# The gates of a linear recurrence: both gates of a head side by side in one stationary operand, two heads in the two row halves of TensorE, tanh on 64 partitions at a time

## The reference

```python
def block_diag_linear(x, w, b):            # 16 heads of 64 channels
    xb = x.reshape(bsz, s, LRU_BLOCKS, LRU_BLOCK_W)
    y = jnp.einsum('bsnc,ncd->bsnd', xb, w).reshape(bsz, s, LRU_WIDTH)
    return y + b

def rg_lru(x, w_a, b_a, w_x, b_x, lam):
    r = jax.nn.sigmoid(block_diag_linear(x, w_a, b_a))
    i = jax.nn.sigmoid(block_diag_linear(x, w_x, b_x))
    log_a = -LRU_C * r * jax.nn.softplus(-lam)
    a = jnp.exp(log_a)
    mult = jnp.sqrt(jnp.maximum(-jnp.expm1(2.0 * log_a), 0.0))
    bterm = mult * (i * xf)
    # h[t] = a[t] * h[t-1] + bterm[t]
```

## Time and profile before

| what | value |
|---|---|
| median of 3 runs | 1322.02 us |
| profiled execution: its own time | 1322.41 us |
| profiled execution: span of the trace | 1320.6 us |
| PE busy | 1309.9 us, 99% of the span |
| DVE busy | 917.7 us, 69% |
| ACT busy | 716.3 us, 54% |
| moved by DMA | 233.36 MB, 177 GB/s in the mean |
| load of `lru_w` | one transfer of 1024.0 KB |

### The profile page before, as it was taken

One profiled execution on the slowest core, in us unless ns is written; L12 is line 12 of the kernel. 1 busy time (PEld: TensorE's weight loads), 2 busy tenths in 40 slices (PEclk: granted clock), 3 DMA queues, 4 the chain that ended last, 5 costly groups with the idle time before them and its releaser, 6 DMA issues.

```text
span 1320.6 us, 18090 instructions
## 1 busy us (share of the span) xinstructions
PE 1309.9 (99%) x7220; PEld 1113.3 (84%) x7220; DVE 917.7 (69%) x1113; ACT 716.3 (54%) x1021; POOL 94.1 (7%) x84
## 2 busy tenths in 40 slices
PE   9999999999999999999999999999999999999999
PEld 7788888987788888888888999888888889998887
DVE  6756556687978755546767668876776766698675
ACT  6544445568746544435776444554467664445452
POOL 0000000000101000001252000000002610000000
PEclk9999999999999999999999999999999999999999
DMA  7866637542386866545656543546566564344562
GB/s 262 281 212 199 205 111 243 172 127 81 128 255 207 268 187 187 189 143 159 206 162 199 168 129 115 190 144 181 185 199 216 174 208 145 113 144 144 150 196 85
DMA packets 64243, 233.36 MB, mean 177 GB/s; under 512 B 7456, under 2 KB 7584, under 8 KB 64032
## 3 DMA queue, kind: packets, MB, share of 16 engines
q1 hardware_dynamic: 61488, 223.37, 53.9%
q10 hardware_dynamic: 2672, 8.84, 2.0%
HBM read 231.14 MB, written 1.05 MB: 176 GB/s over the span
## 4 chain that ended last, share of the span: by engine, by line
PE 89%; DVE 5%; DMA 2%; ACT 2%; issue 1%; POOL 1%; ACTq 0%; another core or an unknown queue 0%; POOLq 0%; DVEq 0%
PE psum L1906 22%; PE psum L1927 22%; PE psum L1907 22%; PE psum L1974 5%; PE psum L1912 5%; PE psum L1959 5%; PE psum L1913 5%; PE psum L2122 2%; DMA raw<-weights 2%; PE psum L2345 2%; DVE w_lo L1173 1%; DVE y_lo L1173 1%; PE psum L2223 1%; ACT w_hi L606 0%; ACT y_hi L606 0%
## 5 line engine op out<-in xcount | busy, mean ns | idle before, releaser
L1173 DVE TENSOR_TENSOR w_lo<-raw,w_hi 128x1024 fp32r<-128x1024 f32 x226 | 274.1, 1222 | 125.9 <-ACT w_hi L606 124.1
L606 ACT ACTIVATE w_hi<-raw 128x1024 fp32r<-128x1024 f32 x226 | 237.7, 1057 | 139.9 <-PE psum L1927 104.3
L1906 PE MATMUL psum<-w_hi,x_hi 128*128 128x512 f32 x552 | 218.3, 396 | 1.0 <-ACT w_hi L606 1.0
L1173 DVE TENSOR_TENSOR y_lo<-raw,y_hi 128x1024 fp32r<-128x1024 f32 x144 | 175.3, 1222 | 58.8 <-ACT y_hi L606 57.9
L1907 PE MATMUL psum<-w_hi,x_lo 128*128 128x512 f32 x552 | 214.9, 389 | 0.0
L606 ACT ACTIVATE y_hi<-raw 128x1024 fp32r<-128x1024 f32 x144 | 151.9, 1057 | 80.9 <-PE psum L1927 49.4
L1927 PE MATMUL psum<-w_lo,x_hi 128*128 128x512 f32 x552 | 170.2, 389 | 0.3 <-DVE w_lo L1173 0.3
L1906 PE MATMUL psum<-y_hi,x_hi 128*128 128x512 f32 (+1 forms) x376 | 148.6, 395 | 0.0
L1907 PE MATMUL psum<-y_hi,x_lo 128*128 128x512 f32 (+1 forms) x376 | 146.5, 390 | 0.0
L1906 PEld LDWEIGHTS psum<-w_hi,x_hi 128*128 128x128 f32 x552 | 103.9, 188 | 24.4 <-issue 2.6
L1927 PEld LDWEIGHTS psum<-w_lo,x_hi 128*128 128x128 f32 x552 | 103.7, 188 | 22.6 <-DVE w_lo L1173 1.2
(11 more groups left out here) (204 smaller groups left out, 2327.4 us busy)
## 6 DMA issues: line engine op xcount, KB each, us to landing
raw<-weights SPq DMA_DIRECT2D x422, 512.0 KB, 4.0
arena<-gains ACTq DMA_DIRECT2D x7, 512.0 KB, 4.7
arena<-gate_bias ACTq DMA_DIRECT2D x2, 1536.0 KB, 8.0
res<-x SPq DMA_DIRECT2D x2, 512.0 KB, 5.8
arena<-lru_w ACTq DMA_DIRECT2D x1, 1024.0 KB, 4.8
cst<-consts ACTq DMA_DIRECT2D x1, 736.0 KB, 5.4
out<-res SPq DMA_DIRECT2D x1, 512.0 KB, 2.6
out<-res SPq DMA_DIRECT2D x2, 256.0 KB, 2.0
```

What stands on the lines that cost most here:

```text
L606: act.activation(slot(t)[0], raw[:, t % RAW, :], ACT.Copy).then_inc(hi_ready, 1)
L1173: dve.tensor_tensor(lo, raw[:, t % RAW, :], hi.bitcast(F32), ALU.subtract).then_inc(lo_ready, 1)
L1906: pe.matmul(out_, l_hi, r_hi, start=start, stop=False, skip_group_check=skip)
```

## The change

The stationary operand becomes 128 partitions x 8 feature tiles x 128 columns: on the 64 rows of a head lie its r matrix (64 columns) and its i matrix (64 columns). A matmul takes 64 rows and streams the head's 64 channels x 256 tokens; its result has r on partitions 0 to 63 and i on 64 to 127 for one head. The two heads of a feature tile are in the upper and lower row half and write to the two banks of a pair. A part is now two feature tiles with both gates, no longer four feature tiles with one gate. The counts of matmuls, and of parts, stay.

ACT now has four reads for a feature tile: for each gate and head, 64 partitions x 256. Where gate and head lie in other halves, it writes to other partitions than it reads. Before the decays it waits for its own reads of both parts. The biases are laid out anew, and `lru_w` is half as large.

```diff
-        lru_blocks = view(0, 2, KD, P)
+        lru_blocks = view(0, KD, P)
...
-            act.dma_start(lru_blocks.rearrange("p a f d -> p (a f d)"), lru_w).then_inc(lru_loaded, 16)
+            act.dma_start(lru_blocks.rearrange("p f d -> p (f d)"), lru_w).then_inc(lru_loaded, 16)
...
-            def tanh_part(half, which):
-
-                act.wait_ge(ri_ready, 2 * half + which + 1)
-                fill = (F_R0, F_I0, F_R1, F_I1)[2 * half + which]
-                dst = lru_i if which else lru_a
-                for j in range(4):
-                    f = 4 * half + j
-                    ins = act.activation(dst[:, f, :], pair(fill)[:, j // 2, (j % 2) * SEQ:(j % 2 + 1) * SEQ],
-                                         ACT.Tanh, scale=0.5, bias=half_bias[:, which * KD + f:which * KD + f + 1])
+            def tanh_part(half, part):
+
+                act.wait_ge(ri_ready, 2 * half + part + 1)
+                fill = (F_R0, F_I0, F_R1, F_I1)[2 * half + part]
+                for f in range(4 * half + 2 * part, 4 * half + 2 * part + 2):
+                    for dst, rows in ((lru_a, slice(0, HEAD)), (lru_i, slice(HEAD, P))):
+                        for i in range(2):
+                            ins = act.activation(dst[HEAD * i:HEAD * (i + 1), f, :],
+                                                 pair(fill)[rows, i, (f % 2) * SEQ:(f % 2 + 1) * SEQ], ACT.Tanh,
+                                                 scale=0.5, bias=half_bias[rows, i * KD + f:i * KD + f + 1])
                 ins.then_inc(act_freed, 1)
 
             def decay_tanh(half):
 
+                act.wait_ge(*freed((F_I0, F_I1)[half]))
                 for f in range(4 * half, 4 * half + 4):
...
-                for which in range(2):
-                    fill = (F_R0, F_I0, F_R1, F_I1)[2 * half + which]
+                for part in range(2):
+                    fill = (F_R0, F_I0, F_R1, F_I1)[2 * half + part]
                     fill_ready(fill)
-                    for j in range(4):
-                        f = 4 * half + j
-                        ins = pe.matmul(pair(fill)[:, j // 2, (j % 2) * SEQ:(j % 2 + 1) * SEQ],
-                                        lru_blocks[:, which, f, :], xc[:, f, :], start=True, stop=True)
+                    for f in range(4 * half + 2 * part, 4 * half + 2 * part + 2):
+                        for i in range(2):
+                            head = slice(HEAD * i, HEAD * (i + 1))
+                            ins = pe.matmul(pair(fill)[:, i, (f % 2) * SEQ:(f % 2 + 1) * SEQ], lru_blocks[head, f, :],
+                                            xc[head, f, :], start=True, stop=True)
                     ins.then_inc(ri_ready, 1)
```

More of the change, by code:

```diff
@@ L2586 @@
         + [columns(named["conv_w"][0, k]) for k in range(CONV1)]
-        + [columns(named[n][0]) for n in ("conv_b", "lru_b_a", "lru_b_x", "lru_lambda")]
+        + [columns(named["conv_b"][0])]
+        + [np.concatenate([named[n][0].reshape(KD, 2, HEAD)[:, i].T for n in ("lru_b_a", "lru_b_x")]) for i in range(2)]
+        + [columns(named["lru_lambda"][0])]
         + [np.broadcast_to(named["attn_sinks"][0][head_order()], (P, Q_HEADS))], 1)
@@ L2590 @@
         "ffn1_post_g", "mix_post_g", "ffn2_post_g", "mix_pre_g", "ffn2_pre_g")] + list(named["norm_g_2"])])
-    lru_w = np.zeros((P, 2, KD, P), np.float32)
-    for a, name in enumerate(("lru_w_a", "lru_w_x")):
-        w = named[name][0]
-        for f in range(KD):
-            for i in range(2):
-                part = slice(HEAD * i, HEAD * (i + 1))
-                lru_w[part, a, f, part] = w[2 * f + i]
-    lru_w = lru_w.reshape(P, -1)
+    lru_w = np.stack([named[n][0] for n in ("lru_w_a", "lru_w_x")], 2)
+    lru_w = lru_w.reshape(KD, 2, HEAD, 2 * HEAD).transpose(1, 2, 0, 3).reshape(P, D)
     layer_params = np.stack([np.concatenate(
```

## The result

| | kernel before | changed kernel |
|---|---|---|
| median | 1321.98 us (4 runs, 1321.80 to 1323.14) | 1330.13 us (4 runs, 1329.66 to 1330.82) |
| profiled execution: span | 1320.6 us | 1328.4 us |
| mean granted clock of PE | 1.000 | 0.997 |

The changed kernel is 8.15 us slower. The ratio of the times is 1.006, with a 95% interval of 1.0043 to 1.0078. The forecast was 1324.2 us, with a range up to 1327.0: the direction was right, the size and the range were not.

The account below looks back on a forecast made before the run. PE's stream was taken as the bound, with ACT's first-part gate reads holding the chunk behind the gates: +1.11 us per half, +2.2 us in all, other terms 0, giving 1324.2 us, range 1321.4 to 1327.0.

Parts of the forecast that it names:

- the two first parts, read in eight: ACT's tanh reads of the first gate part, both halves: eight instead of four make PE +1.11 us late per half.
- ACT's longer stream behind them: ACT's 16 extra reads, 2.9 us per chunk, hidden in chunks 7 and 8 with 0.5 and 0.2 us to spare.
- the granted clock: PE's clock behind the gate waits: the sum gave it no cost; a fall to 1.2 GHz was only a rival, 0.04.
- What bounds the kernel: PE's stream sets the time, but the dense chunk behind the gates starts 0.05 us after ACT's first-part reads.
- PE's part: Gate matmuls: two parts take 2.1 us instead of 3.55 per half; the second still waits for F_GATE1 or F_GL0.
- The step of ACT's reads, 0.36: Gate tanh reads of 64 partitions start 0.36 us apart, as with 128, so eight take 3.0 us.
- The forecast's formula: Delay over both halves for a read step s: 2 x (-0.33 + 8 s - 4 x 0.36).
- The bounds: Step of ACT's gate reads: 0.18 us if 64 partitions cost half, 0.48 if changing partitions breaks the overlap.
- rival 2: ACT's gate reads cost more than 0.36 us each: 1325.5 at step 0.42, 1326.9 at 0.48; chance 0.14.
- Rival 4: PE's clock falls to 1.2 GHz behind idles of 0.7 and 1.8 us at the gates: 1330 us; chance 0.04.
- the four cases: The rivals: PE's gain arrives (0.08), dearer ACT reads (0.14), row halves not side by side (0.05), slower clock (0.04).
- The new wait, `lru_w`, other engines: Wait before `decay_tanh` met long before; 512 KB less of `lru_w` worth 0; DVE, POOL, SP get no new instruction.

Follow-up runs that it names:

- second profile: The changed kernel, unedited, timed and profiled again on another call's chip: 1330.18 us, ratio 1.0057.
- second part whole, PE busy: Changed kernel with the second gate part's matmuls issued three times, and that part read by four tanh of 128 partitions instead of eight reads: 1326.41 us, ratio 1.0029.
- PE busy: Changed kernel with the four matmuls of the second gate part issued three times over, ACT's reads unchanged: 1327.51 us, ratio 1.0038.
- split reads in alternating order: Kernel before with each 128-partition tanh read of the gates split into two of 64, lower half then upper: 1328.66 us, ratio 1.0042.
- result's half fixed: Changed kernel with a part's eight reads ordered by the half they write, the half read changing every time: 1329.01 us, ratio 1.0048.
- reads in pairs: Changed kernel with reads of equal source and result halves paired: 1328.05 us, ratio 1.0037; with PE's second-part matmuls also repeated: 1325.91 us, ratio 1.0027.

## Why the prediction was wrong

The loss in the mixer, at the third mark, can be taken apart in two ways: by the runs that remove one part after another, or by the changed kernel's own trace. The numbers in brackets are of its second profile.

| step | forecast | by runs | in its own trace |
|---|---|---|---|
| the two first parts, read in eight | +2.2 | +3.8 (second part whole, PE busy) | +3.9 |
| ACT's longer stream behind them | 0 | +1.5 (PE busy, less the row above) | 0 |
| the granted clock | 0 | +1.6 (+2.9) (changed kernel, less PE busy) | +3.1 (+4.4) |
| sum | +2.2 | +6.95 (+8.27) | +6.95 (+8.3) |

In the changed kernel's trace the chunk behind the gates starts 1.93 us late in half 0 (288.33 from a start of 281.01, for 286.00 from 280.61), 1.95 more in half 1, and from there to the values it takes 1.58 and 1.50 us longer, at the lower clock. That is all of the 6.95 us. ACT's longer stream holds nothing there: ACT still waits 0.88 us for DVE before its exponentials, and PE waits 0.20 us at chunk 9's scores, for 0.18 before.

```profile
296.99 0.40 ACT L776 ACTIVATE probs<-probs,scores_max 128x128 f32<-128x128 f32 x1 [0.88 <-DVE sum_recip L1566]
...
328.49 1.13 PE L2124 MATMUL psum<-arena 64*128 64x256 f32 x8 [0.20 <-DVE probs_t L1353]
```

The two ways don't contradict each other. PE at the lower clock gives ACT time to catch up; take the fall of the clock away, and 1.5 us of the gain go to waits for ACT. The split reads in alternating order show the same: where the clock stayed up, in half 1, PE waits 1.10 us at chunk 9's scores, and 0.88 us is lost between the second and the third mark.

- **What bounds the kernel; PE's part.** Right. A part took 1.1 us, the dense chunk went on 0.05 us behind ACT's last read, and PE's gain alone was worth 0.65 us (0.66 forecast).
- **The step of ACT's reads, 0.36.** This is the term that was mis-sized: it measured 0.48. From the first read's start to the last one's end that makes 2 x (-0.33 + 3.83 - 1.57) = +3.9, against 3.8 measured. The forecast's formula gives +4.1 for 0.48: it counts eight steps against four, but the last read's 0.48 us doesn't grow with the step, so it takes 0.12 us too much per half. The bounds held it at their upper end, with the reason named (a change of partitions breaks the overlap), but I chose by the nearest row on partition count, and the count turned out not to matter. What mattered, that consecutive instructions change their range, no row showed. The Trainium skill, page "ScalarE: Activation LUTs", section "What ACT_TABLE_LOAD costs", has an overlap of 93 ns for back-to-back instructions without a condition, from tiles of 128 partitions. That the overlap (0.12 us here) is there only for equal ranges, and that 64 partitions take as long as 128, is what these runs add.
- **ACT's longer stream, 0.** It is 0 in the changed kernel, but only because the slow clock covers it; that is luck. With the clock kept up, in the busy run, it costs 1.5 us. One place was named: at a step of 0.48 rival 2 had +0.8 us for DVE's mask, which is about what that run shows between its second and third mark (0.9). Missed was the other place, the exponentials of chunk 7, which had 0.5 us to spare at a step of 0.36 and come 0.6 us late at 0.48.
- **The clock.** This is the term that the sum put at nothing. Rival 4, given 0.04, came in together with rival 2. I priced it against idle stretches of 0.7 and 1.8 us, as the forecast step gave them. They were 0.54 and 2.6. I took the four cases for alternatives, and they are not: the dearer the read, the longer PE idles, and the clock fell behind all six waits of 2.58 or 2.59 us that the runs have. No row stood behind the price of 3 us per half. The first profile's two slow stretches cost 1.58 and 1.50 us in the dense tile behind the gates (from its first matmul to the next tile's, scores and values between them: 6.64 and 6.53 us for 5.06 and 5.03). In the second profile the same waits cost 1.59 and 2.84, the latter from 309.24 to 316.10 in place of 4.02 us:

```profile
309.24 0.80 PE L1908 MATMUL psum<-w_hi,x_hi 128*128 128x512 f32 x1 [2.58 <-ACT arena L848]
...
316.10 1.08 PE L2176 MATMUL psum<-probs_t,arena 128*64 128x512 f32 x4
```

- **The range** to 1327.0 was made from ACT's dearest step alone, and left out the rival that the dearest step brings with it.
- **The new wait, `lru_w`, other engines.** Right as far as the chain of waits of the changed kernel shows: neither the new wait before the decays nor a DMA piece holds anything between 280 and 330 us.

What stays open: what makes the granted clock fall behind one wait and not behind another of nearly the same length (below), and what makes a slow stretch cost 1.5 us once and 2.8 another time. By the latter the second half of the changed kernel lost 3.45 us in one profile and 4.8 in the other.

## What to carry to other kernels

Before cutting one engine's work, look who releases its next instruction: here PE's gates ended together with ACT's read of them, so a 40% cut on PE was worth 0.65 us, and what the change added to the reads that PE waits for was paid in full. Rivals that share a cause belong in one case: here a longer wait of PE and a lower clock came together, and the price was their sum. What a part costs also depends on which others are there: ACT's longer stream cost nothing beside the slow clock and 1.5 us without it. And when many small instructions follow each other on an engine, order them so that neighbours have the same partitions; the same eight reads took 3.12 or 3.83 us per part by their order alone.

## What the runs showed of the hardware

- ACT's tanh from PSUM, 256 elements with a pointer bias: starts 0.36 us apart where source and result keep their partition ranges, 0.48 where either changes; 64 partitions cost as much as 128.
- The granted clock behind a wait of PE (the idle time that PE's row names, in us): it fell behind each of 2.58 or 2.59, behind two of 2.10, and behind 2.06 and 2.01, and stayed at 1.00 behind 1.99, 1.37, 1.34, 1.30, 0.85, 0.37 and 0.33. The kernels differ in what PE did ahead of the wait too, so this is no threshold.
- What a fall of the clock cost up to the values of its chunk: 1.50 to 1.59 us in eight of the ten falls, 2.71 and 2.84 in the other two (half 1 with the result's half fixed, and half 1 of the changed kernel's second profile).
- Matmuls that compute nothing new, issued into such a wait, kept the clock at 1.00 in all three kernels that had them. They were worth 1.6 us at the third mark against the changed kernel's first profile, 2.9 against its second, and 2.6 with the reads in pairs (6.02 to 3.41).
